# Index scores: the keys' low part against 64 rows of the array instead of 128

## The reference

```python
dots = jnp.einsum('bqhd,bsd->bqhs', qi, k_idx).astype(jnp.float32) * IDX_DIM ** -0.5
score = jnp.einsum('bqhs,bqh->bqs', jax.nn.relu(dots), wi)
score = jnp.where(visible[None], score, -jnp.inf)
top_val, top_idx = lax.top_k(score, n_sel)
```

## Time and profile before

| | |
|---|---|
| median of 3 runs | 1594.09 us (1594.06 to 1594.47) |
| profiled execution | 1594.46 us |
| its span, first to last instruction | 1592.8 us |
| mean granted TensorE clock | 0.998 |
| busy share of PE, PEld, DVE, ACT | 99%, 82%, 53%, 36% |
| matmuls, of them index scores | 7106, 96 |

### The profile page before, as it was taken

How to read it: one execution, slowest core, us unless ns; L and a number is a source line. 1 busy time by engine, 2 the same in 40 slices (tenths; PEclk the granted TensorE clock), 3 DMA queues, 4 the chain that set the end, 5 groups by cost and what they waited for, 6 DMA issues and landing times.

```text
span 1592.8 us, 19975 instructions
## 1 busy us (share of the span) xinstructions
PE 1582.4 (99%) x7106; PEld 1313.2 (82%) x7106; DVE 837.9 (53%) x1231; ACT 572.6 (36%) x851; POOL 15.8 (1%) x35
## 2 busy tenths in 40 slices
PE   9999999999999999999999999999999999999997
PEld 7788888888888888888888888888888888888886
DVE  5853678522126655556665546564556544434333
ACT  5542333222224444334453333343332533323232
POOL 0000000000000000000000000000000000000000
PEclk9999999999999999999999999999999999999999
DMA  7223223332333333333334333333333522253223
GB/s 221 87 80 93 85 88 93 97 100 81 105 106 96 108 106 107 113 114 97 112 117 130 113 102 112 99 117 110 115 94 117 187 97 92 100 203 119 99 100 119
DMA packets 97979, 176.39 MB, mean 111 GB/s; under 512 B 11264, under 2 KB 24080, under 8 KB 97296
## 3 DMA queue, kind: packets, MB, share of 16 engines
q1 hardware_dynamic: 93712, 160.60, 33.3%
q0 software_dynamic: 3040, 13.63, 2.3%
q10 hardware_dynamic: 1184, 1.58, 0.3%
HBM read 156.90 MB, written 8.39 MB: 104 GB/s over the span
## 4 chain that ended last, share of the span: by engine, by line
PE 97%; ACT 1%; DVE 1%; issue 0%; ACTq 0%; DVEq 0%
PE proj L1199 29%; PE proj L1200 29%; PE proj L1198 29%; PE attn L1199 3%; PE attn L1200 3%; PE attn L1198 3%; PE attn L1333 1%; PE attn L1332 1%; ACT junk L466 0%; PE proj L1260 0%; ACT w_hi L413 0%; DVE w_lo L724 0%; PE attn L1247 0%; PE attn L1365 0%; DVE xs L767 0%
## 5 line engine op out<-in xcount | busy, mean ns | idle before, releaser
L1198 PE MATMUL proj<-u_hi,w_hi 128*128 128x512 f32 x1536 | 598.9, 390 | 0.5 <-DVE u_lo L777 0.5
L1199 PE MATMUL proj<-u_lo,w_hi 128*128 128x512 f32 x1536 | 598.4, 390 | 0.0
L1200 PE MATMUL proj<-u_hi,w_lo 128*128 128x512 f32 x1536 | 598.3, 390 | 0.0
L724 DVE TENSOR_TENSOR w_lo<-stage,w_hi 128x1024 fp32r<-128x1024 f32 x266 | 323.4, 1223 | 444.3 <-ACT w_hi L413 443.0
L413 ACT ACTIVATE w_hi<-stage 128x1024 fp32r<-128x1024 f32 x266 | 280.1, 1056 | 426.0 <-PE proj L1200 296.2
L1198 PEld LDWEIGHTS proj<-u_hi,w_hi 128*128 128x128 f32 x1536 | 288.7, 188 | 60.6 <-issue 1.3
L1200 PEld LDWEIGHTS proj<-u_hi,w_lo 128*128 128x128 f32 x1536 | 288.5, 188 | 60.3
L1199 PEld LDWEIGHTS proj<-u_lo,w_hi 128*128 128x128 f32 x1536 | 288.6, 188 | 59.2
L1200 PE MATMUL proj<-w_hi,u_lo 128*128 128x512 f32 x256 | 99.7, 389 | 0.0
L1199 PE MATMUL proj<-w_lo,u_hi 128*128 128x512 f32 x256 | 99.6, 389 | 0.0
L1198 PE MATMUL proj<-w_hi,u_hi 128*128 128x512 f32 x256 | 99.6, 389 | 0.0
(11 more groups left out here) (189 smaller groups left out, 1414.5 us busy)
## 6 DMA issues: line engine op xcount, KB each, us to landing
stage<-in_w_in SPq DMA_DIRECT2D x208, 512.0 KB, 3.7
stage<-in_w_out SPq DMA_DIRECT2D x32, 512.0 KB, 3.6
x_in<-turned SPq DMA_DIRECT2D x256, 40.0 KB, 1.9
stage<-in_w_branch_sb SPq DMA_DIRECT2D x16, 512.0 KB, 3.7
stage<-in_w_branch_sa SPq DMA_DIRECT2D x16, 512.0 KB, 4.1
xs<-in_x SPq DMA_DIRECT2D x8, 512.0 KB, 8.0
o_scratch<-og POOLq DMA_DIRECT2D x16, 256.0 KB, 2.3
hres<-in_x POOLq DMA_DIRECT2D x1, 4096.0 KB, 14.2
```

The lines of the kernel that those rows point to most:

```text
L724: V.tensor_tensor(w_lo[:, s % RING, :, :], stage[:, s % 2, :, :], w_hi[:, s % RING, :, :].bitcast(F), ALU.subtract).then_inc(strip_lo, 1)
L1198: nc.tensor.matmul(out_, a_hi, b_hi, start=start, stop=False, skip_group_check=free)
L1199: nc.tensor.matmul(out_, a_hi, b_lo, start=False, stop=False, skip_group_check=free)
L1200: return nc.tensor.matmul(out_, a_lo, b_hi, start=False, stop=stop, skip_group_check=free)
```

## The change

In each step of `dots` the two matmuls over all 128 rows with `kix_hi` come first, one for each head, and open their banks (`start=True`). Then come the two matmuls with `kix_lo`. They now take 64 rows of the array each: the partitions on which the head has its high part, rows 0 to 63 for the even head and rows 64 to 127 for the odd one. They close the banks and raise `dots_done`. The product q_lo*k_lo is no longer in the sum. The number of matmuls, their columns and the banks stay.

```diff
-                        o_ = attn[h % 4][:, 0:WQ[qi]]
-                        nc.tensor.matmul(o_, q, kix_lo[:, 0:WQ[qi]], start=True, stop=False)
-                        nc.tensor.matmul(o_, q, kix_hi[:, 0:WQ[qi]], start=False, stop=True).then_inc(dots_done, 1)
+                        nc.tensor.matmul(attn[h % 4][:, 0:WQ[qi]], q, kix_hi[:, 0:WQ[qi]], start=True, stop=False)
+
+                    for h, rows_ in zip((2 * s, 2 * s + 1), HALVES):
+                        nc.tensor.matmul(attn[h % 4][:, 0:WQ[qi]], area_r[rows_, 16 + h, P * qi:P * qi + P],
+                                         kix_lo[rows_, 0:WQ[qi]], start=False, stop=True).then_inc(dots_done, 1)
```

## The result

The changed kernel takes 1599.49 us (median of 7 runs, 1599.32 to 1600.33) against 1594.12 us of the kernel before in the same comparison (median of 7, 1594.06 to 1594.8). The ratio is 1.0034, with a 95% interval of 1.0024 to 1.0043: 5.4 us slower. Its seven runs have a granted clock of 0.998 or 0.999, the profiled one of before 0.998. The forecast was 1595.1 us, the range 1591.0 to 1600.6. The time lies in the range, but in the slow rival's part of it, 1597.7 to 1600.3 us. The profiled execution has a span of 1597.8 us, 5.0 us more than before.

The account below looks back on a forecast made before the run. TensorE's stream, the distances between matmul starts, was taken to bound the kernel. Overlap -1.6 us and shape changes +2.6 us gave +1.0 us: 1595.5 us against the profiled execution, a median of 1595.1 us; range 1591.0 to 1600.6 us.

Parts of the forecast that it names:

- slow rival: At both shape changes of a step, exposed loads, emptying or both: 1597.7, 1600.3 or 1605.5 us; chance 0.38.
- What bounds the kernel: TensorE's own stream: distances between matmul starts set the time; the 24 steps take 16.7 us, 1% of the kernel.
- The overlap: Two narrow matmuls of a step run at once, the second 0.108 us behind the first: gain 1.6 us.
- utmost case: Both narrow loads of a step run at the same time and the second matmul costs nothing: gain 4.2 us.
- The change of shape: Array going from 128 rows to 64 and back, 48 times: one exposed load a step, 24 x 0.108 = 2.6 us.
- The bounds: Price of one change of array shape: nothing if loads run ahead, up to 0.27 us if emptying and load add up.
- the threshold in the rival: Price for each change of array shape above which the kernel is slower by over 3.2 us: 0.10 us.
- the array empties: Slower rival at both shape changes of a step: exposed loads, emptying, or both, +3.6 to +11.4 us; chance 0.38.
- case of two exposed loads: A load exposed at both shape changes of a step: -1.6 + 5.2 = +3.6 us, 1597.7 us; chance 0.20 near it.
- that of both: At each shape change the array empties and the load comes on top: +11.4 us, 1605.5 us.
- 0.163 us for the emptying: At each shape change, the rest of a matmul's life beyond its distance, 0.390 - 0.228 us; 48 of them give +6.2 us.
- The signs of being wrong: In the profile after: narrow matmuls lasting longer than full ones, a falling granted clock, or PE waiting for ACT.

Follow-up runs that it names:

- order only: Against the changed kernel, both lo matmuls on all 128 rows, keeping the order hi, hi, lo, lo: 1594.12 us against 1594.33 for the kernel before, ratio 0.9999.
- same half: Against the changed kernel, both narrow matmuls on rows 0 to 63, so they can't overlap: 1603.78 us against 1594.33 for the kernel before, ratio 1.0060.

## Why the prediction was right or wrong

**What bounds the kernel: right.** 5.2 of the 5.4 us lie in the 24 steps, by the distances between matmuls; ACT, DVE and the transfers have no part in it. ACT's relus waited 95.7 us instead of 89.9, at no cost to PE, and moving the first head's `dots_done` cost nothing (order only, ratio 0.9999).

**The overlap: right in kind, the term too small.** The prediction took the second narrow matmul 0.108 us behind the first, a gain of 1.6 us, "since it is what the rows show of when loads are issued". It was the utmost case: 4.2 us, with both narrow loads at once. The steps of before show only full loads, which follow one another; two narrow ones for different halves take 0.19 us together, and two for the same half 0.29. With 256 keys the loads were to leave almost no gain. That fell with it: two narrow loads together take the time of one. The Trainium skill (TensorE: Matmul & The Clock Gate, Part 3: Packing small matmuls) says about 4 ns between such starts. The trace agrees within what it resolves, 0.50 us for the pair against 497 ns for one.

**The change of shape: the step that failed.** "I take one exposed load a step, not two: at one of the two changes it will not run ahead" priced 24 x 0.108 = 2.6 us. The runs showed 48 x 0.197 = 9.5 us: the load is exposed at both changes, alike in both directions, and before each there is another 0.08 to 0.10 us, behind the last column of the old shape, in which nothing is loaded. The bounds were 0 and 0.27 us a change, and 0.197 lies between; the threshold in the rival, 0.10 us a change, was right for the gain of 1.6 us, and was passed. So "the array empties" is what happened, between its case of two exposed loads (+3.6 us) and that of both (+11.4 us), with a gain larger than it counted. Its 0.163 us for the emptying, read from the length of a record, was nearly twice what passes before the load. That the wait before the load is the array emptying fits its place, behind the last column of the old shape, and that it is the same for all widths; the records do not show the array itself, so this much is argued. The Trainium skill (TensorEngine Tiling (Array Packing), Key Properties) says that a change of tiling mode drains the engine. The trace agrees in where the wait stands; 0.197 us is what a change costs here, the exposed load with it.

**The two errors stood against each other**: 2.6 us too little gain and 6.9 us too little price leave 4.3, and the forecast of +1.0 became +5.4. That the time still lies in the range is luck in part: with the price as measured and the gain as forecast it would have been -1.6 + 9.5 = +7.9 us, 1602.0, beyond the range. The earlier trace rows had leaned the right way, a full load 0.18 us behind a narrow matmul; I set it aside as a single instance at a slower stage. The earlier trace rows had been misread as weak evidence for a cheap change: those transposes are on all 128 rows and make no change of shape at all. Their exposed load is only the pace of loads: the load of L1198 comes at 12.64, behind the eight others, and the one after it at 12.75.

**The signs of being wrong.** The prediction called itself wrong in kind if narrow matmuls last longer than full ones. By the records they do, 497 ns against 388, and still the sign means nothing: it took the record for the work, and a narrow matmul whose load went ahead is recorded with 393 ns (same half). The other two signs, a lower granted clock and a wait of PE for ACT, did not come.

## What to carry to other kernels

Two matmuls on different halves of the array run in the time of one, their weight loads too, but every change between 128 rows and 64 or 32 costs some 0.2 us on TensorE's stream. Narrow matmuls pay only in runs long enough to save more than 0.4 us each: here a run of two pairs of 512 columns just breaks even. When a price is missing in a trace, ask whether the load behind a change can still be issued ahead. Here none of another shape was, and 48 exposed loads of 0.108 us, 5.2 us, are by themselves more than the 4.2 us that the overlap could give.

## What the hardware showed that was not expected

- The price is the same into the narrow shape and out of it, for 256, 384 and 512 columns (0.193 to 0.198 us), and for 64 and 32 rows (+5.4 and +5.6 us).
- Matmuls on 96 rows among full ones pay no such price: +0.5 us, with a ratio of 1 inside the interval, and loads ahead as always.
- Of two halves, the loads as well as the matmuls run at once (two loads in 0.19 us, one takes 0.18).
- The record of a matmul whose load has not gone ahead is about 0.10 us longer than that of one whose load has (0.50 against 0.39): it starts with its load. Read as durations, these records would put a slower matmul where there is an exposed load.
